# Copying attention's results later, and on VectorE in one chunk, with the gated rows turned one slot later

## The chip, the cores and the metric

The kernel runs on one core of a Trainium2 chip. The metric is the device time of one execution in microseconds (us); lower is better.

## What is computed

Two residual layers on 1024 tokens with 1024 features, in float32. The first is a pooling mixer with a gate. The second, which matters here, is dilated attention with 8 heads of 128 and three groups g of dilations (1, 4, 16):

```python
q = rotary(rms_norm(qkv[:, :, g, 0], q_norm[g]), pos, ROPE_DIM, ROPE_THETA)
k = rotary(rms_norm(qkv[:, :, g, 1], k_norm[g]), pos, ROPE_DIM, ROPE_THETA)
o, lse = dilated_window_attention(q, k, qkv[:, :, g, 2], dil, window // (2 * dil))
...
weights = jax.nn.softmax(jnp.stack(lses, axis=0), axis=0)
o = jnp.einsum('gbsh,gbshe->bshe', weights, jnp.stack(outs, axis=0))
y = o.reshape(B, S, ATT_WIDTH).astype(h.dtype) * jax.nn.silu(gate)
return y @ w_out
```

## The kernel before

All projections come first; attention starts at about 1361 us of the span and lasts to the end. It is cut into six chunks, each of four heads (a half) and one group, in the order `CHUNKS = ((0, 0), (1, 0), (0, 1), (0, 2), (1, 1), (1, 2))`. A chunk has 8 query blocks of 128 rows. A *step* t is one query block of a chunk (t from 0 to 47, and eight more to drain); it has four *slots* h, one for each head, numbered n = 4t + h. The fourth chunk is steps 24 to 31. Its group needs one key block for each query block; groups 0 and 1 need two.

Every engine runs the same loop over n, in an order written out by hand, and waits on semaphores. In slot n TensorE turns the probabilities of head n-3 (L1489, `transpose_p`), makes the scores of head n (L1481, `scores`; called S in the text) and the value product of head n-4 (L1509, `values`). VectorE copies the turned probabilities of head n-3 out of PSUM (L2162, `take_pt`), then adds the mask and takes the row maximum of head n (L2153, `row_max`). ScalarE takes the exponential of head n (L2672, `exps`).

Around that, once in a step: TensorE turns the next step's queries (slot 0) and a block of the next chunk's keys (slot 2, in steps 33 to 38 slot 3), both at L1439 and both into PSUM bank 2; ScalarE copies them out (`take_queries` L2616, `take_keys` L2664) in the same slots, behind the exponential. ScalarE copies the results of a step, four heads in one PSUM bank of 512 columns, to SBUF (`take_u`, L2686).

A half is merged when its third chunk is there. From step 34 (rows 0 to 7) and step 44 (rows 8 to 15) on, one row block m a step is merged: VectorE weighs (L2201) and GpSimd adds and gates (from m = 12 on VectorE and ScalarE do it). One step later TensorE turns the gated rows, also into bank 2 (`turn_gated`, L1439 with `turn` or `turnh_f` as the source); ScalarE copies this out rounded (`y_high`, L2699), VectorE writes the remainder (`y_low`, L2222). One step after that come two half products with the output weight (`project_out`, in slots 0 and 2, 12 products of 512 columns each), which VectorE adds to the residual (L2231). The products of rows 6 and 7 are spread over slot 0 of steps 42 to 45 instead, so these steps have none in slot 2; nor has step 35. ScalarE (L2707) and VectorE (L2237) also split the output weights in steps 40 to 44, and in steps 42, 44, 46 and 48 they make merging factors.

A turn into bank 2 waits until the last contents are copied out:

```python
def bank2_free():
    for ready, n in zip((kt_copied, qt_copied, ylo_done), turned):
        if n:
            pe.wait_ge(ready, n)
```

Of the kernel before, what the change touches and what calls it, by code (L numbers as in the profile page):

```python
# [37 lines left out]
def encoder_program(nc, x, pool_norm, pool_w_in, pool_w_group, pool_scale, pool_w_out, att_norm, att_w_in,  # L38
# [3 lines left out]
    TB, KD = T // P, D // P  # L42
# [92 lines left out]
    with ctx:  # L135
# [332 lines left out]
        def group(c):  # L468

            return CHUNKS[c][1]  # L470
# [46 lines left out]
        def row_at(t, lag):  # L517

            found = [m for m in range(NROW) if merge_step(m) + lag == t]
            return found[0] if found else None  # L520
# [28 lines left out]
        def spill_number(c, b):  # L549

            return TB * [n for n in range(NCHUNK) if CHUNKS[n][1] < NA - 1].index(c) + b

        ON_POOL = range(TB + 4)
        ON_SCALAR = range(TB + 4, NROW)

# [7 lines left out]
        def projected(t, h):  # L563

            if (t, h) in SPREAD:
                return SPREAD[t, h]
            m = row_at(t, 2)
            return (m, h // 2) if h in (0, 2) and m is not None and m not in SPREAD_ROWS else None
# [615 lines left out]
        def _(pe):  # L1184
# [308 lines left out]
            def values(n):  # L1493
                c, h, b = block_of(n)
                t = n // HALF
                if h == 0:
                    if b == 0 or (b == 4 and c == NCHUNK - 1):
                        before_now = [x for x in range(c + 1) if x % 2 == c % 2]
                        wide = sum(CHUNKS[x][1] == 0 for x in before_now)
                        if b == 0:  # L1500
                            pe.wait_ge(v_in[c % 2][0], 16 * len(before_now))
                        if b == 4 or c < NCHUNK - 1:
                            pe.wait_ge(v_in[c % 2][1], 16 * (len(before_now) + 2 * wide))
                    if t >= 2:
                        pe.wait_ge(u_evac, t - 1)
                pe.wait_ge(pt_ready, n + 1)
                vb = value_blocks(group(c), b)
                for i, v in enumerate(vb):
                    last = nc.tensor.matmul(value_bank(t)[:, P * h:P * h + P], pt[:, n % 4, P * i:P * i + P],  # L1509
                                            v_rows[c % 2][v // 4][:, v % 4, HD * h:HD * h + HD], start=(i == 0),  # L1510
                                            stop=(i == len(vb) - 1))
                last.then_inc(pv_done, 1)
# [36 lines left out]
            for n in range(HALF * END):  # L1549
                t, h = n // HALF, n % HALF  # L1550
                if 0 <= n - LAG < NHEAD:
                    transpose_p(n - LAG)
                if n < NHEAD:
                    scores(n)
                if 0 <= n - LAG - 1 < NHEAD:
                    values(n - LAG - 1)
                if projected(t, h):
                    project_out(*projected(t, h))
                if h == 1 and row_at(t, 1) is not None:
                    turn_gated(row_at(t, 1))  # L1560
                if h == 0 and t + 1 < NSTEP:
                    turn_queries(t + 1)
                if h == keys_head(t) and t + TB < NSTEP:
                    turn_keys(t // TB + 1, t % TB)
# [3 lines left out]
        def _(dve):  # L1568
# [587 lines left out]
            def take_pt(n):  # L2156
# [4 lines left out]
                    dve.wait_ge(pv_done, n - 3)  # L2161
                nc.vector.tensor_copy(pt[:, n % 4, 0:kn], bank(3 + n % 2)[:, 0:kn]).then_inc(pt_ready, 1)  # L2162

            def factor_terms(half, first, n):

                at = slice(first, first + n)
                s = [st0[:, half, at], st1[:, half, at], stat[:, last_chunk(half), at]]
                for g in range(2):
                    dve.wait_ge(st_in[g], 16 * (half + 1))
                dve.wait_ge(p_done, HALF * (TB * last_chunk(half) + first + n))  # L2170
                link(nc.vector.tensor_tensor(fmin[:, at, :], s[0][:, :, 0, :], s[1][:, :, 0, :], ALU.min))
                link(nc.vector.tensor_tensor(fmin[:, at, :], fmin[:, at, :], s[2][:, :, 0, :], ALU.min))
                for g in range(NA):
                    last = nc.vector.tensor_tensor(fac[:, g, at, :], fmin[:, at, :], s[g][:, :, 0, :], ALU.subtract)
                last.then_inc(f_sub, 1)
# [64 lines left out]
            for n in range(HALF * END):  # L2240
                t, h = n // HALF, n % HALF
                if projected(t, h - 1):
                    add_rows(*projected(t, h - 1))
                if 0 <= n - LAG < NHEAD:
                    take_pt(n - LAG)
                if n < NHEAD:
                    row_max(n)
                if h == 0 and t in FACTORS:
                    factor_terms(*FACTORS[t])
                if h == 2 and row_at(t, 1) is not None:  # L2250
                    y_low(row_at(t, 1))
                if row_at(t, 0) is not None:
                    merge(row_at(t, 0), h)
                if h == 3 and t in FACTORS:
                    factors(*FACTORS[t])
                if n - 2 in OUT_SPLITS:
                    out_low(OUT_SPLITS[n - 2])
# [3 lines left out]
        def _(act):  # L2261
# [413 lines left out]
            def take_u(t):  # L2675

                c, b = t // TB, t % TB
                act.wait_ge(pv_done, HALF * (t + 1))
                if group(c) == NA - 1:
                    place = v_rows[1][b // 4][:, b % 4, :]  # L2680
                else:
                    n = spill_number(c, b)
                    if n >= 4:
                        act.wait_ge(u_out[n % 4], 16 * (n // 4))
                    place = ub[:, n % 4, :]
                nc.scalar.activation(place, value_bank(t), ACT.Copy).then_inc(u_evac, 1)  # L2686
# [34 lines left out]
            for n in range(HALF * END):  # L2721
                t, h = n // HALF, n % HALF
                if n < NHEAD:
                    exps(n)
                if h == 1 and row_at(t, 1) is not None:
                    y_high(row_at(t, 1))
                if h == 0 and row_at(t, 0) in ON_SCALAR:
                    scale_heads(row_at(t, 0), 3)
                if h > 0 and row_at(t, -1) in ON_SCALAR:
                    scale_heads(row_at(t, -1), h - 1)  # L2730
                if h == 0 and t + 1 < NSTEP:
                    take_queries(t + 1)
                if h == 1 and t in FACTORS:
                    exp_factors(*FACTORS[t])
                if h == 3 and 1 <= t <= NSTEP:
                    take_u(t - 1)
                if h == keys_head(t) and t + TB < NSTEP:
                    take_keys(t // TB + 1, t % TB)
                if n in OUT_SPLITS:
                    out_high(OUT_SPLITS[n])  # L2740
# [52 lines left out]
```

## Time and profile before

| what | value |
|---|---|
| runs | 1683.63 us median of 3 (1682.88 to 1683.65) |
| profiled execution | 1682.04 us, span 1680.2 us |
| TensorE matmul busy | 1656.5 us, 99% of the span |
| VectorE, ScalarE, GpSimd busy | 1148.6, 837.6, 269.6 us |
| granted TensorE clock | 1.0 |

The profile follows one execution; times of rows are us from the start of its span. "Busy" of TensorE uses modelled ends of products. The idle time in brackets at the end of a row is what the engine stood idle ahead of it, and what released it. PE is TensorE, DVE VectorE, ACT ScalarE, POOL GpSimd, SPq the queue of SyncE that issues the transfers.

### The profile page before, as it was taken

How to read it: one execution, taken by the hardware profiler on the slowest of the kernel's cores; microseconds unless marked ns; L12 is line 12 of the kernel's file. 1: busy time of each engine (PE TensorE's matmuls, PEld its weight loads, DVE VectorE, ACT ScalarE, POOL GpSimd, SP SyncE). 2: the span in 40 equal slices, each digit the busy share in tenths (PEclk: the TensorE clock that was granted, in tenths of full speed). 3: DMA queues.
4: the chain of work that ended last, by engine and by line, in shares of the span. 5: the costliest groups of instructions: out<-in, count | busy, mean ns of one | idle time of the engine just before them, and what ended most of it. 6: DMA issues, size and time to landing. Idle time of an engine off the chain costs nothing.

```text
span 1680.2 us, 23792 instructions
## 1 busy us (share of the span) xinstructions
PE 1656.5 (99%) x8294; PEld 1404.1 (84%) x8294; DVE 1148.6 (68%) x1962; ACT 837.6 (50%) x1948; POOL 269.6 (16%) x292
## 2 busy tenths in 40 slices
PE   8999999999999999999999999999999999999999
PEld 8888888778888878888888888888888889999877
DVE  5885677677985687586868356774468336666575
ACT  6453333432441463475655246573456268885453
POOL 2000000004312100141423013240023000004440
PEclk9999999999999999999999999999999999999999
DMA  6133333484411424332332414332334646767774
GB/s 191 51 125 127 123 102 101 151 321 155 175 49 52 143 103 145 106 120 83 125 117 84 155 61 155 107 114 88 125 112 140 230 165 220 251 212 228 256 264 156
DMA packets 146276, 243.12 MB, mean 145 GB/s; under 512 B 17264, under 2 KB 55152, under 8 KB 145136
## 3 DMA queue, kind: packets, MB, share of 16 engines
q1 hardware_dynamic: 141264, 224.31, 39.9%
q10 hardware_dynamic: 4896, 17.30, 2.8%
q8 instruction: 68, 1.11, 0.3%
q14 instruction: 48, 0.39, 0.1%
HBM read 161.75 MB, written 79.82 MB: 144 GB/s over the span
## 4 chain that ended last, share of the span: by engine, by line
PE 91%; DVE 4%; DMA 2%; issue 1%; ACT 1%; SPq 0%; ACTq 0%; POOL 0%; DVEq 0%
PE pair L1186 26%; PE pair L1188 26%; PE pair L1187 26%; PE pair L1509 4%; PE pair L1481 3%; PE pair L1439 3%; PE pair L1489 2%; DMA ubuf<-diff_spill 1%; DMA raw<-in_pool_w_out_dram 1%; PE pair L1207 1%; DMA xs<-in_x_dram 0%; DMA raw<-in_pool_w_in_dram 0%; DVE w L1586 0%; DVE w L1669 0%; DVE hTl L1757 0%
## 5 line engine op out<-in xcount | busy, mean ns | idle before, releaser
L1186 PE MATMUL pair<-w,turnh 128*128 128x512 f32 x640 | 249.0, 389 | 0.0
L1187 PE MATMUL pair<-w,turnh 128*128 128x512 f32 x640 | 249.0, 389 | 0.0
L1188 PE MATMUL pair<-w,turnl 128*128 128x512 f32 x640 | 249.0, 389 | 0.0
L1186 PE MATMUL pair<-w,hTh 128*128 128x512 f32 x544 | 214.0, 393 | 2.2 <-DVE xs L1675 2.2
L1188 PE MATMUL pair<-w,hTl 128*128 128x512 f32 x544 | 212.0, 390 | 0.0
L1187 PE MATMUL pair<-w,hTh 128*128 128x512 f32 x544 | 211.7, 389 | 0.0
L2591 ACT ACTIVATE both<-pair 128x512 f32<-128x512 f32 x160 | 94.3, 592 | 177.8 <-PE pair L1188 166.9
L2089 DVE TENSOR_TENSOR both<-pair,both 128x512 f32<-128x512 f32 x120 | 81.5, 686 | 112.0 <-PE pair L1188 111.4
L2602 ACT ACTIVATE dump<-both 128x128 f32<-128x128 f32 x384 | 119.4, 311 | 64.0 <-DVE both L2089 51.4
L1186 PEld LDWEIGHTS pair<-w,turnh 128*128 128x128 f32 x640 | 120.1, 188 | 25.0
L1187 PEld LDWEIGHTS pair<-w,turnh 128*128 128x128 f32 x640 | 120.1, 188 | 25.0
L1188 PEld LDWEIGHTS pair<-w,turnl 128*128 128x128 f32 x640 | 120.1, 188 | 24.9
L1154 POOL TENSOR_SCALAR qvar<-qss 128x4 f32<-128x4 f32 x96 | 41.5, 432 | 539.8 <-ACT dump L2602 536.9
L1186 PEld LDWEIGHTS pair<-w,hTh 128*128 128x128 f32 x544 | 102.2, 188 | 22.9 <-DVE xs L1675 2.5
L1188 PEld LDWEIGHTS pair<-w,hTl 128*128 128x128 f32 x544 | 102.1, 188 | 21.5
L2672 ACT ACTIVATE pp<-pp,stat 128x256 f32<-128x256 f32 (+2 forms) x192 | 86.8, 452 | 66.4 <-DVE stat L2153 64.9
L1187 PEld LDWEIGHTS pair<-w,hTh 128*128 128x128 f32 x544 | 102.2, 188 | 20.6
L2162 DVE COPY pt<-pair 128x256 f32<-128x256 f32 (+1 forms) x192 | 72.5, 378 | 50.3 <-PE pair L1489 47.0
L1142 POOL TENSOR_TENSOR diff<-stage,diff 128x1024 fp32r<-128x1024 f32 x12 | 42.3, 3556 | 388.9 <-ACT diff L2486 388.9
L1159 POOL TENSOR_TENSOR qrstd<-qvar,neg_half 128x4 f32<-128x4 f32 x96 | 100.9, 1051 | 8.0
L1186 PE MATMUL pair<-hTh,w 128*128 128x512 f32 (+1 forms) x280 | 99.5, 355 | 2.7 <-DVE hTl L1757 1.9
L1187 PE MATMUL pair<-hTl,w 128*128 128x512 f32 (+1 forms) x280 | 98.7, 353 | 0.0
(241 smaller groups left out, 3819.1 us busy)
## 6 DMA issues: line engine op xcount, KB each, us to landing
part_spill<-both SPq DMA_DIRECT2D x160, 256.0 KB, 3.6
both<-part_spill SPq DMA_DIRECT2D x22, 1024.0 KB, 6.6
raw_z<-in_att_w_in_dram SPq DMA_DIRECT2D x20, 1024.0 KB, 5.3
raw<-in_pool_w_in_dram SPq DMA_DIRECT2D x32, 512.0 KB, 5.7
raw<-in_att_w_in_dram SPq DMA_DIRECT2D x10, 1024.0 KB, 6.2
raw_u<-in_att_w_in_dram SPq DMA_DIRECT2D x10, 1024.0 KB, 5.7
diff_spill<-ubuf SPq DMA_DIRECT2D x16, 512.0 KB, 2.6
stage<-gate_spill SPq DMA_DIRECT2D x16, 512.0 KB, 6.1
```

The costliest lines, as they stand in the source:

```text
L1159: nc.gpsimd.tensor_tensor(qrstd[:, z % 4, :], qvar[:, z % 4, :], neg_half[:, :], ALU.pow).then_inc(a_rstd, 1)
L1186: nc.tensor.matmul(out, lh, rh, start=first, stop=False, skip_group_check=onto)
L1187: nc.tensor.matmul(out, lh, rl, start=False, stop=False, skip_group_check=onto)
L1188: return nc.tensor.matmul(out, ll, rh, start=False, stop=last, skip_group_check=onto)
L1439: last = nc.tensor.transpose(out[:, P * h:P * h + P], rows[:, P * h:P * h + P], ident[:, :])
L1481: nc.tensor.matmul(out, qT[:, b % 2, h, :], keys(c, b, h), start=True, stop=True).then_inc(s_done, 1)
L1509: last = nc.tensor.matmul(value_bank(t)[:, P * h:P * h + P], pt[:, n % 4, P * i:P * i + P], v_rows[c % 2][v // 4][:, v % 4, HD * h:HD * h ...
L2089: nc.vector.tensor_tensor(place, bank(source), place, ALU.add).then_inc(a_added, 1)
L2162: nc.vector.tensor_copy(pt[:, n % 4, 0:kn], bank(3 + n % 2)[:, 0:kn]).then_inc(pt_ready, 1)
L2591: nc.scalar.activation(place, bank(4 + p if i == 3 else p), ACT.Copy).then_inc(a_kept, 1)
L2602: nc.scalar.activation(dump[:, :], x4[:, h, :], ACT.Square, accum_out=qss[:, z % 4, h:h + 1]).then_inc(a_sq, 1)
L2672: nc.scalar.activation(pp[:, n % 4, at], pp[:, n % 4, at], ACT.Exp, bias=stat[:, c, b, 0, h:h + 1], scale=-1.0, accum_out=stat[:, c, b, 1, ...
```

## The change

The copy of a step's results stands at slot 3 of the next step; it now stands at slot 1 of the step after that. In the fourth chunk (`ON_VECTOR`) VectorE makes it, behind its row maximum. `turn_gated` moves from slot 1, behind the output product if there is one, to slot 2, ahead of it, and `y_high` from slot 1 to slot 2, behind the exponential; `y_low` was in slot 2 already.

```diff
+        ON_VECTOR = range(TB * CHUNKS.index((0, NA - 1)), TB * CHUNKS.index((0, NA - 1)) + TB)
...
                     values(n - LAG - 1)
+                if h == 2 and row_at(t, 1) is not None:
+                    turn_gated(row_at(t, 1))
                 if projected(t, h):
                     project_out(*projected(t, h))
-                if h == 1 and row_at(t, 1) is not None:
-                    turn_gated(row_at(t, 1))
...
+            def take_u(t):
+
+                b = t % TB
+                dve.wait_ge(pv_done, HALF * (t + 1))
+                if t == ON_VECTOR.start:
+                    dve.wait_ge(u_evac, t)
+                nc.vector.tensor_copy(v_rows[1][b // 4][:, b % 4, :], value_bank(t)[:, :]).then_inc(u_evac, 1)
...
                     row_max(n)
+                if h == 1 and t - 2 in ON_VECTOR:
+                    take_u(t - 2)
...
                 act.wait_ge(pv_done, HALF * (t + 1))
+                if t == ON_VECTOR.stop:
+                    act.wait_ge(u_evac, t)
...
-                if h == 1 and row_at(t, 1) is not None:
+                if h == 2 and row_at(t, 1) is not None:
                     y_high(row_at(t, 1))
...
-                if h == 3 and 1 <= t <= NSTEP:
-                    take_u(t - 1)
+                if h == 1 and 2 <= t <= NSTEP + 1 and t - 2 not in ON_VECTOR:
+                    take_u(t - 2)
```

How this stands on the engines, at the three places of which the text below speaks. The lines of the changed kernel are up to 13 numbers higher.

VectorE in a step of the fourth chunk, before the change, slots 1 and 2: a copy of turned probabilities, and a row maximum in two instructions.

```order
L2162 COPY pt<-pair 128x128
L2153 ISA pp,stat<-pair,both 128x128
L2153 ISA stat 128x1
L2162 COPY pt<-pair 128x128
L2153 ISA pp,stat<-pair,both 128x128
```

The same place in the changed kernel (`turn` is where the group's results go).

```order
L2163 COPY pt<-pair 128x128
L2154 ISA pp,stat<-pair,both 128x128
L2154 ISA stat 128x1
L2171 COPY turn<-pair 128x512
L2163 COPY pt<-pair 128x128
L2154 ISA pp,stat<-pair,both 128x128
```

The 512 column copy has come between the row maximum of slot 1 and the copy of slot 2.

TensorE in step 42 before: the query turn that ends slot 0, slot 1 with the gated turn, slot 2.

```order
L1439 MATMUL pair<-ident,both 128x128 x4
L1489 MATMUL pair<-ident,pp 128x128
L1481 MATMUL pair<-turnh_f,qT 128x128
L1509 MATMUL pair<-turn,pt 128x128
L1439 MATMUL pair<-ident,turnh_f 128x128 x4
L1489 MATMUL pair<-ident,pp 128x128
L1481 MATMUL pair<-turnh_f,qT 128x128
L1509 MATMUL pair<-turn,pt 128x128
```

And now.

```order
L1440 MATMUL pair<-ident,both 128x128 x4
L1490 MATMUL pair<-ident,pp 128x128
L1482 MATMUL pair<-turnh_f,qT 128x128
L1510 MATMUL pair<-turn,pt 128x128
L1490 MATMUL pair<-ident,pp 128x128
L1482 MATMUL pair<-turnh_f,qT 128x128
L1510 MATMUL pair<-turn,pt 128x128
L1440 MATMUL pair<-ident,turnh_f 128x128 x4
```

The gated turn has moved behind the second head.

ScalarE in step 42 before, from the exponential of slot 1 on: y_high, the factors' exponential, a weights' copy, the exponentials of slots 2 and 3, the results copy.

```order
L2672 ACTIVATE pp,stat<-pp,stat 128x128
L2699 ACTIVATE hTh<-pair 128x512
L2692 ACTIVATE fac<-fac 128x3x8
L2707 ACTIVATE turnl<-raw 128x512
L2672 ACTIVATE pp,stat<-pp,stat 128x128 x2
L2686 ACTIVATE turn<-pair 128x512
```

And now (here L2699 is the results copy and L2712 is y_high).

```order
L2683 ACTIVATE pp,stat<-pp,stat 128x128
L2705 ACTIVATE fac<-fac 128x3x8
L2699 ACTIVATE turn<-pair 128x512
L2720 ACTIVATE turnl<-raw 128x512
L2683 ACTIVATE pp,stat<-pp,stat 128x128
L2712 ACTIVATE hTh<-pair 128x512
```

y_high has moved behind the exponential of slot 2, and the results copy has come ahead of both.

## Rows read from the trace of the kernel before

**Rows 1.** Stretch, length, busy us (xcount) of PE, PEld, DVE, ACT, POOL; clock, DMA.

```profile
1440.00:1480.00 40.00, 40.00 (x330) 39.76 (x328) 26.35 (x107) 32.16 (x93) 0.00 (x0) 1.00 0.69 228
1500.00:1510.00 10.00, 9.43 (x83) 8.95 (x81) 6.62 (x36) 9.73 (x32) 0.00 (x0) 1.00 0.53 185
```

**Rows 2.** Timeline, fourth chunk, one period: start, duration, engine, instruction.

```profile
1492.60 0.63 PE L1439 MATMUL pair<-ident,both 128*128 128x128 f32 x4 [0.19 <-issue]
1493.18 0.39 PE L1481 MATMUL pair<-turnh_f,qT 128*128 128x128 f32 x2
1493.27 0.69 ACT L2664 ACTIVATE turn<-pair,lead 128x512 f32<-128x512 f32 x1
1493.71 0.29 DVE L2153 CUSTOM_DVE_ANT_0 pp<-pair,both 128x128 f32<-128x128 f32 x1
1494.05 0.40 ACT L2672 ACTIVATE pp<-pp,stat 128x128 f32<-128x128 f32 x1
1494.18 0.60 PE L1439 MATMUL pair<-ident,both 128*128 128x128 f32 x4
1494.45 0.58 ACT L2686 ACTIVATE turn<-pair 128x512 f32<-128x512 f32 x1
1495.31 0.67 ACT L2616 ACTIVATE qT<-pair,lead 128x512 f32<-128x512 f32 x1
1496.08 0.63 PE L1439 MATMUL pair<-ident,both 128*128 128x128 f32 x4 [0.19 <-issue]
```

**Rows 3.** Timeline, VectorE: copies of 128 and of 256 columns.

```profile
1499.30 0.29 DVE L2162 COPY pt<-pair 128x128 f32<-128x128 f32 x1
1499.51 0.28 DVE L2153 CUSTOM_DVE_ANT_0 pp<-pair,both 128x128 f32<-128x128 f32 x1
...
1517.35 0.42 DVE L2162 COPY pt<-pair 128x256 f32<-128x256 f32 x1
```

**Rows 4.** Timeline, last keys' copy ahead of the fifth chunk, its first scores.

```profile
1510.65 0.69 ACT L2664 ACTIVATE turn<-pair,lead 128x512 f32<-128x512 f32 x1
1511.44 0.56 PE L1481 MATMUL pair<-turn,qT 128*128 128x192 f32 x2 [0.16 <-issue]
```

**Rows 5.** Timeline, steps 33 and 34: results copy, keys' copy, query turn.

```profile
1520.46 0.58 ACT L2686 ACTIVATE ub<-pair 128x512 f32<-128x512 f32 x1
1520.94 0.68 ACT L2664 ACTIVATE turnh_f<-pair,lead 128x512 f32<-128x512 f32 x1
...
1521.67 0.55 PE L1439 MATMUL pair<-ident,both 128*128 128x128 f32 x3 [0.34 <-ACT turnh_f L2664]
```

**Rows 6.** Timeline, step 35: VectorE's weighing, y_low, key turn.

```profile
1526.71 1.96 DVE L2201 TENSOR_TENSOR both<-both,fac 128x1024 f32<-128x1024 f32 x1
...
1530.37 0.69 DVE L2222 TENSOR_TENSOR hTl<-pair,hTh 128x512 fp32r<-128x512 f32 x1
...
1531.31 0.63 PE L1439 MATMUL pair<-ident,both 128*128 128x128 f32 x4 [0.16 <-issue]
```

**Rows 7.** Timeline, step 42: query turn, exponential, gated turn, value product.

```profile
1598.08 0.60 PE L1439 MATMUL pair<-ident,both 128*128 128x128 f32 x4
...
1599.49 0.40 ACT L2672 ACTIVATE pp<-pp,stat 128x128 f32<-128x128 f32 x1
1599.51 0.63 PE L1439 MATMUL pair<-ident,turnh_f 128*128 128x128 f32 x4 [0.27 <-issue]
...
1601.86 0.35 PE L1509 MATMUL pair<-turn,pt 128*128 128x128 f32 x1 [0.28 <-DVE pt L2162]
```

**Rows 8.** Timeline, step 45: exponential of slot 2, value product behind slot 3.

```profile
1621.07 0.40 ACT L2672 ACTIVATE pp<-pp,stat 128x128 f32<-128x128 f32 x1 [0.33 <-DVE stat L2153]
...
1621.98 0.46 PE L1509 MATMUL pair<-turnh_f,pt 128*128 128x128 f32 x2 [0.28 <-DVE pt L2162]
```

**Rows 9.** Timeline, step 48: value product of slot 2.

```profile
1644.37 0.49 PE L1509 MATMUL pair<-turnh_f,pt 128*128 128x128 f32 x2 [0.17 <-DVE pt L2162]
```

**Rows 10.** The statistics' tile: time from issue to landing of its four loads.

```profile
DMA to landing us min/median/max: 2.2/6.6/7.7
```

## The prediction

> **What bounds the kernel now.** I read the stretches first. While the third chunk runs (1440 to 1480 us) TensorE is busy in all of its 40 us and ScalarE in 32; in the fourth chunk (1500 to 1510) TensorE shows 9.43 of 10 and ScalarE 9.73 [rows 1]. So nearly everywhere TensorE's own work is the time, and only its waits can be changed; both edits lie in the last 190 us. Then I read the timeline, one step at a time, and looked on TensorE for turns and value products that carry an idle time. The ends of its products are modelled, so the idle printed is smaller than the stall; I take stalls from the starts.
>
> The fourth chunk has one key block for each query block. From a key turn at 1492.60 to the query turn at 1494.18 TensorE needs 1.58 us (a turn and two heads; a turn is about 0.45, a head 0.56); from there to the next key turn, the same work, it takes 1.90 [rows 2]. The 0.32 is a stall. What closes the circle of 3.48 us (1492.60 to 1496.08) is ScalarE: key turn, S 0.58 later, VectorE's row maximum 0.53 later, exponential 0.34, copy of the results 0.40, then exponential and copy of the queries 0.86 after that copy began, whose 0.67 us end releases the key turn [rows 2]. The results copy L2686 is on this circle with some 0.47 us.
>
> **The change, part by part.** Of the fourth chunk's copies, eight go from ScalarE to VectorE; all others stay on ScalarE and move from slot 3 to slot 1 of the next step, where nothing waits for them in chunks 1 to 3, since TensorE is full there [rows 1]. No instruction is added but waits.
>
> (a) *Fourth chunk.* VectorE has no row for a copy of 512 columns from PSUM. Its copies of 128 and 256 columns last 0.29 and 0.42, 0.13 for 128 more; after one of 128 the next instruction starts 0.21 later [rows 3], so one of 512 holds the queue for 0.21+3x0.13 = 0.60 (0.68 if all of its duration counts: the upper bound; 0.5, if its cost per column were a little less, the lower). The new copy stands in slot 1 behind the row maximum; queued behind it are the probabilities' copy and the row maximum of slot 2, behind these ScalarE's exponential of slot 2 and its copy of the keys, and TensorE's next query turn waits for that copy, as both turns use bank 2. The circle that this makes: query turn to S of slot 1 0.58, to row maximum 0.53, to the new copy 0.21, to the probabilities' copy 0.60, to the maximum 0.21, to the exponential 0.34, to the keys' copy 0.40 [rows 2, 3], to the query turn 0.73 (1520.94 to 1521.67) [rows 5]: 3.60 us. That is more than the 3.48 of now. ScalarE's relief is real, but the last arrival is now the keys' copy instead of the queries'. Five periods (steps 26 to 31) cost 5x0.12 = 0.6, the step before some 0.1. At the seam, S of the fifth chunk waits for the last keys' copy: 0.79 after its start [rows 4]. That start is 1.90+0.67 = 2.57 after the query turn now and 3.60-0.73 = 2.87 then: +0.3. Together **+1.0** (0.4 to 1.5 with 3.5 to 3.68 for the circle). [...]
>
> (b) *Steps 33 and 34.* Here the keys are turned in slot 3, and ScalarE's results copy stood ahead of the keys' copy: 1520.46, then 1520.94, then the query turn 1521.67 with a printed wait [rows 5]. Moved away, the keys' copy starts 0.48 earlier: **-0.5**. In step 34 the same wait stands, but VectorE is then inside its 1.96 us product L2201 (from 1526.71) [rows 6], and the value product behind the query turn waits for it: nothing gained (at best another 0.5).
>
> (c) *Step 35.* Turning the gated rows in slot 2 puts ScalarE's y_high behind the exponential of that slot and behind the results copy that now stands in slot 1: 0.47 us for the copy and some 0.45 for the exponential later. y_low starts at 1530.37 now and the key turn that waits for it at 1531.31 [rows 6]. In step 35 there is no output product to cover it: **+0.8** (0.5 to 0.95).
>
> (d) *Steps 36 to 41, and 46.* With an output product of 12 wide matmuls behind the turn, y_high and y_low are covered. What goes: in steps 41, 42, 45 and 46 the gated turn in slot 1 waits for the queries' copy of slot 0. Query turn 1598.08, gated turn 1599.51, 1.43 apart for 1.00 of work [rows 7]; the row stands at 1589.99, 1618.89 and 1626.47 too. 0.43 us each. Steps 41 and 46 keep it, the latter less what a late VectorE copy takes, and 0.1 comes in step 40: **-0.8**. In 42 and 45 it is swallowed by the next term.
>
> (e) *Steps 42 and 45* have a gated turn and no product in slot 2. VectorE then stands in y_low until y_high is done, and the probabilities' copy of slot 3 is queued behind it, for which the value product of the next slot waits. Step 42: ScalarE's exponential of slot 1 starts at 1599.49 [rows 7]; 0.40 for it, 0.2 (an estimate) for that of the factors, 0.47 results copy, 0.6 weights' copy (as wide as that of the results, 0.58 [rows 2]), 0.4 exponential of slot 2 put y_high at 1601.55; y_low 0.62 later (y_high is as wide, too), the copy 0.60 after that, the value product 0.33 after that (0.29 and a semaphore): 1603.1, where it is 1601.86 now [rows 7]: +1.2. Step 45: the exponential of slot 2 starts at 1621.07 because VectorE's maximum does, and this is not changed; 0.40+0.62+0.60+0.33 behind it is 1623.0, now 1621.98 [rows 8]: +1.05. Together **+2.25** (1.5 to 2.6).
>
> (f) *Steps 47 and 48* turn no queries. The value product of slot 2 waits for VectorE there, as at 1644.37 [rows 9], and the gated turn, which filled that wait, now comes behind it: 0.35 (step 47, where less is waited) and 0.45: **+0.8** (0 to 0.9). From step 49 on no heads are left, and the order of turns and products is the old one: nothing.
>
> Sum: 1.0-0.5+0.8-0.8+2.25+0.8 = **+3.5 us**. It is made on an execution of 1682.04 (span 1680.2); the median of the three runs is 1683.63, 1.6 above. On the median: **1687.2 us**.
>
> **Rivals.** *VectorE is never last.* It is busy 6.6 us of 10 in the fourth chunk [rows 1]. If the copy and y_low fit into its idle time, then ScalarE's relief counts in full: the fourth chunk falls to TensorE's own 3.1 to 3.2 us a step (-0.3x6, seam -0.3), -0.5, four gated waits (-1.7): -4.3, 1679.3 us, faster. It decides whether in the fourth chunk the keys' copy starts less than 0.85 after the key turn. Against it: the slack there is small, the keys' copy could start only 0.18 later than now (1493.27+0.73 against 1494.18) [rows 2]. Chance 0.1.
> *The copy is absorbed, the y stalls are not*: with a circle near 3.2, (a) becomes -2, and the sum +0.5: 1684.1. Chance 0.12.
> *The y stalls are small*: if ScalarE reaches y_high early, terms (c) and (e) vanish and 42 and 45 keep their 0.43: sum about -0.4, 1683.2. Against it, ScalarE issues in order and the exponential of slot 2 needs VectorE. Chance 0.1.
> *SyncE's queue.* Step 39's results are now copied in slot 1 of step 41 instead of slot 3 of step 40, and SyncE's last load of the statistics stands behind their store. Such loads landed 2.2 to 7.7 us after their issue [rows 10]; VectorE wants this one in slot 0 of step 42, an estimated 4.5 us after its new issue. With the longest landing it is up to 3 us more, 1690. Chance 0.08.
>
> **Numbers.** My forecast has 0.6, with its own range 1685.3 to 1688.9 from the bounds of (a), (c), (e) and (f), not all at one end. The whole range, 1682.8 to 1689.0, takes in the second and third rival. 0.2% of 1683.63 is 3.4 us, about what a measurement of this kernel tells from no change; the forecast lies on that border. So slower 0.45, same 0.45, faster 0.1.
>
> **What would show it.** (a) In the fourth chunk the idle stands before the query turns, not the key turns, and these are 3.6 us apart; the keys' copy starts about 1.27 after its turn. (b) 1521.67's wait is gone. (c) to (e): no idle before gated turns; VectorE waits for hTh in steps 35, 42 and 45, and the value product behind it idles by over 1.5 us in 42. It would be wrong if VectorE's copy lets the queue go in under 0.5 us, or if some stall of mine is taken up by a wait that stands there anyway.

## The result and the profile after

| | before | changed |
|---|---|---|
| median of 17 runs each, side by side | 1682.91 us (1681.71 to 1684.27) | 1686.95 us (1684.30 to 1688.78) |
| profiled execution, span | 1682.04, 1680.2 us | 1685.22, 1683.4 us |
| matmul, VectorE, ScalarE busy | 1656.5, 1148.6, 837.6 us | 1655.7, 1151.4, 834.7 us |

The ratio is 1.0022 (95% interval 1.0016 to 1.0028): 4.0 us slower in the medians, 3.2 in the two profiled executions, both at a mean granted clock of 1.0. Three executions far off all others are left out of the ranges and ratios below: one each of two variants, at a mean clock of 0.75 and 0.56, and one of the kernel before that took 5555 us. The two differences, 4.0 and 3.2, turn out to have different causes. First the 3.2.

The stretches of [rows 1] in the changed kernel:

```profile
1440.00:1480.00 40.00, 40.00 (x330) 39.77 (x329) 26.30 (x109) 31.96 (x93) 0.00 (x0) 1.00 0.71 235
1500.00:1510.00 10.00, 9.21 (x79) 8.64 (x78) 7.15 (x37) 8.28 (x30) 0.00 (x0) 1.00 0.62 224
```

In the fourth chunk ScalarE has been relieved, by 1.45 us in 10, and TensorE, which is what counts, does less than before. The timeline of one period (beside [rows 2]), with all lines that make up the circle:

```profile
1494.69 0.66 PE L1440 MATMUL pair<-ident,both 128*128 128x128 f32 x4 [0.26 <-ACT turn L2675]
...
1496.04 0.69 DVE L2171 COPY turn<-pair 128x512 f32<-128x512 f32 x1
1496.29 0.60 PE L1440 MATMUL pair<-ident,both 128*128 128x128 f32 x4
...
1496.64 0.28 DVE L2163 COPY pt<-pair 128x128 f32<-128x128 f32 x1
...
1496.84 0.28 DVE L2154 CUSTOM_DVE_ANT_0 pp<-pair,both 128x128 f32<-128x128 f32 x1
...
1497.17 0.40 ACT L2683 ACTIVATE pp<-pp,stat 128x128 f32<-128x128 f32 x1 [0.51 <-DVE stat L2154]
1497.57 0.67 ACT L2675 ACTIVATE turn<-pair,lead 128x512 f32<-128x512 f32 x1
...
1498.29 0.66 PE L1440 MATMUL pair<-ident,both 128*128 128x128 f32 x4 [0.26 <-ACT turn L2675]
```

The new copy lasts 0.69 us, and the next instruction on VectorE starts 0.60 after it. ScalarE now stands idle 0.51 waiting for VectorE's row maximum, the keys' copy is late, and the idle of TensorE has moved from the key turns to the query turns, which are 3.60 us apart.

Steps 34 and 35, the turns and the product on VectorE (beside [rows 5, 6]):

```profile
1522.48 0.66 PE L1440 MATMUL pair<-ident,both 128*128 128x128 f32 x4
...
1527.39 0.66 PE L1440 MATMUL pair<-ident,both 128*128 128x128 f32 x4
1527.52 1.45 DVE L2210 TENSOR_TENSOR both<-both,fac 128x1024 f32<-128x1024 f32 x1
...
1530.99 0.58 ACT L2712 ACTIVATE hTh<-pair 128x512 fp32r<-128x512 f32 x1
1531.60 0.69 DVE L2231 TENSOR_TENSOR hTl<-pair,hTh 128x512 fp32r<-128x512 f32 x1 [1.41 <-ACT hTh L2712]
1532.54 0.63 PE L1440 MATMUL pair<-ident,both 128*128 128x128 f32 x4 [1.04 <-DVE hTl L2231]
```

The two query turns have lost their wait (the second stood at 1527.06 before, below); the key turn behind `y_low` has 1.04 us where it had 0.16.

```profile
1527.06 0.65 PE L1439 MATMUL pair<-ident,both 128*128 128x128 f32 x4 [0.34 <-ACT turnh_f L2664]
```

Step 42 (beside [rows 7]), step 45 ([rows 8]) and the tail ([rows 9]):

```profile
1601.44 0.39 ACT L2683 ACTIVATE pp<-pp,stat 128x128 f32<-128x128 f32 x1
1601.83 0.58 ACT L2712 ACTIVATE hTh<-pair 128x512 fp32r<-128x512 f32 x1
1602.44 0.69 DVE L2231 TENSOR_TENSOR hTl<-pair,hTh 128x512 fp32r<-128x512 f32 x1 [1.53 <-ACT hTh L2712]
1603.05 0.28 DVE L2163 COPY pt<-pair 128x128 f32<-128x128 f32 x1
...
1603.47 0.46 PE L1510 MATMUL pair<-turn,pt 128*128 128x128 f32 x2 [1.89 <-DVE pt L2163]
...
1624.76 0.46 PE L1510 MATMUL pair<-turnh_f,pt 128*128 128x128 f32 x2 [1.41 <-DVE pt L2163]
...
1642.83 0.46 PE L1510 MATMUL pair<-turnh_f,pt 128*128 128x128 f32 x2 [0.41 <-DVE pt L2163]
...
1647.11 0.49 PE L1510 MATMUL pair<-turnh_f,pt 128*128 128x128 f32 x2 [0.61 <-DVE pt L2163]
```

In steps 42 and 45 this is one chain: the exponential of slot 2, the upper half on ScalarE, the lower half on VectorE, the probabilities' copy queued behind it, the value product. In step 35 the same chain ends in the key turn instead, which waits for the lower half. The last two rows are another matter. The wait of 0.41 stands in the kernel before as well, and the 0.61 is the 0.17 of [rows 9], grown because the gated turn that filled part of it now comes behind it.

```profile
1640.09 0.46 PE L1509 MATMUL pair<-turnh_f,pt 128*128 128x128 f32 x2 [0.41 <-DVE pt L2162]
```

The table of TensorE's waits of the whole execution agrees: waits for `pt` 3.2 us before (first line), 6.6 after.

```profile
PE pair L1509 <- DVE pt L2162: 3.2, 8, 1.3
...
PE pair L1510 <- DVE pt L2163: 6.6, 9, 1.9
```

### The profile page after: what moved, and what is told of

Same layout as the page of the kernel before. It is cut to its first block, busy times and chain, and to the rows that moved or that the text cites. A ratio compares the mean times of both kernels' runs of the same rounds, so it can differ in the third digit from the quotient of the medians.

```text
span 1683.4 us, 23793 instructions
## 1 busy us (share of the span) xinstructions
PE 1655.7 (98%) x8294; PEld 1404.1 (83%) x8294; DVE 1151.4 (68%) x1970; ACT 834.7 (50%) x1940; POOL 270.7 (16%) x292
## 4 chain that ended last, share of the span: by engine, by line
PE 91%; DVE 4%; issue 1%; DMA 1%; ACT 1%; SPq 0%; ACTq 0%; POOL 0%; DVEq 0%
PE pair L1187 26%; PE pair L1189 26%; PE pair L1188 26%; PE pair L1510 4%; PE pair L1482 3%; PE pair L1440 3%; PE pair L1490 2%; DMA raw<-in_pool_w_out_dram 1%; PE pair L1208 1%; DMA xs<-in_x_dram 0%; DVE pt L2163 0%; DMA raw<-in_pool_w_in_dram 0%; ACT pp L2683 0%; DVE hTl L1758 0%; DVE w L1587 0%
```

## The experiments

Three batches on three chips. Besides the medians I compare the steps' starts in the traces (by ScalarE's copy of the queries, L2616 and its equals, one a step; "steps 24 to 32" is from the copy in step 24 to that in step 32), and the executions at a mean clock of 1.0, for a reason that the first batch shows. In the 96 runs of the kernel before that stood beside the experiments, 44 had a mean clock of 1.0 (median 1682.0) and 52 of 0.999 (1683.5), none less.

**Copy back on ScalarE.** All copies two steps behind, none on VectorE.

```diff
-                if h == 1 and t - 2 in ON_VECTOR:
-                    take_u(t - 2)
...
-                if h == 1 and 2 <= t <= NSTEP + 1 and t - 2 not in ON_VECTOR:
+                if h == 1 and 2 <= t <= NSTEP + 1:
```

> The changed kernel with the fourth chunk's copies back on ScalarE (slot 1, two steps behind); the gated turn stays in slot 2. Theory 1 (the VectorE copy closes a circle of 3.60 us through the keys' copy, and the gated turn makes the stalls of steps 35, 42 and 45): the period of steps 26 to 31 falls to about 3.45 us (query turn, S 0.58, maximum 0.53, exponential 0.34, results copy 0.40, exponential 0.47, keys' copy 0.40, query turn 0.73), and the kernel stays about 1.9 us over the kernel before: 1684.8. Theory 2 (moving ScalarE's copies to slot 1 is what costs, wherever they are made): no gain over the changed kernel, 1687, and chunks 1 to 3 show waits of TensorE that the kernel before has not.

Measured: 1687.04 (1685.76 to 1687.94), ratio 1.0024 (1.0015 to 1.0034). Steps 24 to 32 took 29.37 us, against 28.73 before and 29.85 in the changed kernel: the steps were 3.46, but for one of 3.82, whose row maximum began 0.36 late for no reason that the trace shows, and the fifth chunk still began late. So of the 1.1 us that the fourth chunk lost, taking the copy off VectorE gives back 0.5, or 0.8 without that one step, but not all. The expectation's second theory, that the place of the copies on ScalarE is what costs, is out: steps 0 to 23 take 116.42 us in all three kernels. But the time, expected at 1684.8, is off by 2.2. At the same mean clock the variant is a little faster than the changed kernel (at 0.999 1686.1 against 1687.0, at 0.998 1687.9 against 1688.3), yet none of its nine executions had 1.0. In this profile the step from the queries' copy of step 42 to that of 43 took 9.59 us, where it took 8.01 in the changed kernel's profile, with the same wait of 1.90 in it.

**Gated turn undone.** `turn_gated` and `y_high` in slot 1 as before, the VectorE copy kept.

```diff
-                if h == 2 and row_at(t, 1) is not None:
-                    turn_gated(row_at(t, 1))
                 if projected(t, h):
                     project_out(*projected(t, h))
+                if h == 1 and row_at(t, 1) is not None:
+                    turn_gated(row_at(t, 1))
...
-                if h == 2 and row_at(t, 1) is not None:
+                if h == 1 and row_at(t, 1) is not None:
                     y_high(row_at(t, 1))
```

> The changed kernel with gated turn and y_high back in slot 1, behind the output product; the VectorE copy stays. Theory 1: the waits at about 1532.5, 1603.5 and 1621.2 to 1624.8 us go back to their old size, and 0.4 us waits ahead of the gated turns return; period of the fourth chunk 3.60 still. Sum against the kernel before +1.1 for the fourth chunk, -1.0 for steps 33 and 34: +0.1 to +0.4, 1683.2. Theory 2 (the copies' place costs everything): 1686 to 1687.

Measured: 1683.10 (1681.92 to 1684.23), ratio 1.0002 (0.9993 to 1.0011), period still 3.60. The loss in the fourth chunk (24 to 32: 29.84) stays, steps 32 to 46 take 111.79 instead of 114.28 (before: 112.80). The moved turn is the larger price; the copies of the other chunks, two steps behind, gain 1.0 in steps 33 to 35.

**Turn moved only where covered.** In slot 2 in steps 36 to 41 and 46, where a half product stands behind it, else in slot 1.

```diff
+        def gated_slot(t):
+            return 2 if projected(t, 2) and t < NSTEP - 1 else 1
...
-                if h == 2 and row_at(t, 1) is not None:
+                if h == 2 and h == gated_slot(t) and row_at(t, 1) is not None:
                     turn_gated(row_at(t, 1))
                 if projected(t, h):
                     project_out(*projected(t, h))
+                if h == 1 and h == gated_slot(t) and row_at(t, 1) is not None:
+                    turn_gated(row_at(t, 1))
...
-                if h == 2 and row_at(t, 1) is not None:
+                if h == gated_slot(t) and row_at(t, 1) is not None:
                     y_high(row_at(t, 1))
```

> The changed kernel, but the gated turn and y_high stand in slot 2 only in steps in which an output product follows there (36 to 41 and 46), and in slot 1 in all others. Theory 1: the losses of 42 and 45 (1.2 us each in the profile after) and of step 35 go, the gain of step 41 (0.5) and of 46 (0.3) stays: 0.5 to 1.0 us under the kernel before in spite of the 3.60 us circle, 1682.2. If the cover of the output product does not matter: the same as with the turn undone.

Measured: 1681.85 (1680.85 to 1683.35), ratio 0.9996 (0.9987 to 1.0005); steps 32 to 46 take 111.00. Where the cover is there, the moved turn is a gain: 0.8 us in these steps of the trace, and 0.2 more in step 46 (from there to the last addition 51.11 us, 51.35 with the turn undone).

**VectorE copy in slot 2** instead of slot 1, ahead of slot 3's queue and behind the row maximum for which the keys' copy waits.

```diff
-                if h == 1 and t - 2 in ON_VECTOR:
+                if h == 2 and t - 2 in ON_VECTOR:
                     take_u(t - 2)
```

> The changed kernel with VectorE's copy one slot later, behind the row maximum of slot 2, where TensorE turns the keys. Theory 1: neither the exponential of slot 2 nor that of slot 0 is behind the copy now; the period falls to 3.1 to 3.2 us, the fourth chunk is 2 us faster than in the kernel before instead of 1.1 slower, and the kernel comes out at 1683.0 to 1683.8, since the gated turn's stalls stay. Rival (VectorE's queue is simply too full in this chunk, wherever the copy stands): period 3.5 to 3.6 and no change, 1687.

Measured: 1684.37 (1682.92 to 1686.73), ratio 1.0009 (1.0 to 1.0018); 1683.8 at a clock of 1.0, the top of what was expected. The period is 3.18, TensorE's own work, and steps 24 to 32 take 27.28. Nearly a microsecond of it is given back in steps 33 and 35 (4.33 and 9.92 us, 3.97 and 9.30 in the changed kernel). In step 35 VectorE's product (L2210) lasts 2.08 us instead of 1.45, and the value product behind the query turn waits:

```profile
1528.52 0.49 PE L1510 MATMUL pair<-turn,pt 128*128 128x128 f32 x2 [0.41 <-DVE pt L2163]
```

And this profile, too, has 9.60 us from step 42 to 43. Here is why. TensorE in it behind the wait of step 43, and the stretches around it (length, busy PE, clock, DMA):

```profile
1602.64 0.46 PE L1510 MATMUL pair<-turn,pt 128*128 128x128 f32 x2 [1.89 <-DVE pt L2163]
...
1603.86 0.39 PE L1188 MATMUL pair<-w,hTh 128*128 128x512 f32 x1
1604.09 0.57 PE L1189 MATMUL pair<-w,hTl 128*128 128x512 f32 x1
1604.46 0.63 PE L1187 MATMUL pair<-w,hTh 128*128 128x512 f32 x1
1604.89 0.63 PE L1188 MATMUL pair<-w,hTh 128*128 128x512 f32 x1
```

```profile
1602.00:1604.00 2.00, 1.36 (x7) 1.00 1.03 321
1604.00:1606.00 2.00, 2.00 (x7) 0.53 0.98 322
1606.00:1608.00 2.00, 2.00 (x10) 0.61 0.96 387
1608.00:1610.00 2.00, 2.00 (x20) 1.00 1.06 414
```

The products go from 0.23 to 0.43 us apart: the granted clock has fallen to half, some 1.5 us after the wait ended (in slices of 0.25 us it is 0.50 from 1604.25 to 1607.50, 0.77 and 0.90 in the slices beside, and 1.00 before and behind). The same two stretches in the changed kernel's own profile:

```profile
1604.00:1606.00 2.00, 2.00 (x10) 1.00 0.97 253
1606.00:1608.00 2.00, 2.00 (x18) 1.00 0.98 403
```

So the stall of step 43, which the gated turn of step 42 makes, costs 1.2 us (from step 42 to 43, 8.01 us in the changed kernel's profile for 6.81 before) and in some executions 1.6 more (9.60). There is a second such place in every kernel here, in front of the attention layer's first product, where the kernel before waits, too (2.25 us). In the profile of the variant with the turn where covered (idle 2.27 us ahead of 590.65):

```profile
588.00:590.00 2.00, 0.38 (x4) 1.00 0.67 165
590.00:592.00 2.00, 1.35 (x5) 0.87 1.07 390
592.00:594.00 2.00, 2.00 (x7) 0.50 0.94 268
594.00:596.00 2.00, 2.00 (x13) 0.77 1.02 399
```

and in the kernel before (idle 2.25 us ahead of 591.08), with the clock staying up:

```profile
590.00:592.00 2.00, 0.92 (x4) 1.00 1.03 387
592.00:594.00 2.00, 2.00 (x11) 1.00 0.94 277
594.00:596.00 2.00, 2.00 (x15) 1.00 1.01 376
```

The next eight kernels were chosen for this as much as for the sum.

**Both parts re-placed**: copy in slot 2, turn only where covered.

> The changed kernel with both parts re-placed: VectorE copies the fourth chunk's results in slot 2 instead of slot 1, and the gated row is turned in slot 2 only in the steps where a second half product stands behind it (36 to 41 and 46), in slot 1 in all others. Theory (two independent terms): the copy in slot 2 gave 1.45 us in the fourth chunk against the kernel before, the turn where it is covered 1.8 us over steps 32 to 46 in a profile and 1.0 in the median; together 1680.0 us (1679.3 to 1681.0) where the kernel before has 1682.9. Rival (the two share a gain, since the row that ScalarE is late with after the fourth chunk is the one that the moved turn relieves): 1681.8, no better than the moved turn alone.

Measured: 1681.01 (1679.06 to 1681.60), ratio 0.9988 (0.9979 to 0.9997), the upper end of what was expected. At a clock of 1.0 1679.5, 2.5 below the kernel before, but seven of its ten executions had 0.999. The earlier fourth chunk gives back as much as with the turn in slot 2: in step 35 0.65 (9.02, and 8.37 with the turn alone re-placed), there 0.62. So the terms add.

**Upper half ahead of the exponential** of slot 2 on ScalarE, in all steps.

```diff
+                if h == 2 and row_at(t, 1) is not None:
+                    y_high(row_at(t, 1))
                 if n < NHEAD:
                     exps(n)
-                if h == 2 and row_at(t, 1) is not None:
-                    y_high(row_at(t, 1))
```

> The changed kernel with ScalarE taking the upper half of the turned gated row ahead of the exponential of the same slot 2, instead of behind it, in all steps. Theory (what TensorE waits for in steps 35, 42, 45 and 48 is the chain turn, exponential, upper half, lower half, copy of the turned probabilities, value product): each of these stalls gets shorter by 0.3 to 0.4 us, some of it given back where the exponential is now late in the covered steps: 1685.6 us (1684.8 to 1686.5) where the changed kernel has 1687. Rival (the stall is VectorE's own work, the order on ScalarE does not matter, or the late exponential costs as much): 1687.

Measured: 1683.41 (1683.01 to 1685.66), ratio 1.0007 (0.9998 to 1.0017). The waits of steps 35, 42 and 45 fall:

```profile
1533.68 0.63 PE L1440 MATMUL pair<-ident,both 128*128 128x128 f32 x4 [0.62 <-DVE hTl L2231]
...
1604.29 0.46 PE L1510 MATMUL pair<-turn,pt 128*128 128x128 f32 x2 [1.47 <-DVE pt L2163]
...
1624.75 0.46 PE L1510 MATMUL pair<-turnh_f,pt 128*128 128x128 f32 x2 [0.60 <-DVE pt L2163]
```

By 0.42, 0.42 and 0.81, together 1.65 us; those of 1642.83 and 1647.11 are unchanged. At a clock of 1.0 the variant has 1683.2, 2.0 under the 1685.2 of the changed kernel's seven such executions. The stalls of these three steps are the chain through ScalarE, not VectorE's own work, and the two others are not this chain. The median is below the expected range of 1684.8 to 1686.5, for two reasons. I had put the gain in step 45 too low, since there the exponential itself waited 0.32 us for VectorE. And with 1.47 us of idle none of 11 executions was at 0.998. That alone proves little, as another variant that keeps the 1.89 us (the half copy, below) had one of 11. The profile, taken at a clock of 0.999, had its fall at the second place (0.50 over 592 to 594 us) and 1.00 from 1600 to 1610.

**Stall of step 43 filled** with 14 turns of the identity (their results are overwritten).

```diff
+                if (t, h) == (43, 0):
+                    pe.wait_ge(out_added, 13)
+                    for i in range(14):
+                        nc.tensor.transpose(bank(0)[:, P * (i % 4):P * (i % 4) + P], ident[:, :], ident[:, :])
                 if 0 <= n - LAG - 1 < NHEAD:
                     values(n - LAG - 1)
```

> The changed kernel with 14 turns of the identity (some 1.6 us of TensorE, into the bank that the next half product overwrites) ahead of the value product at which TensorE waits 1.89 us in step 43. Their results are not used. Theory of the clock (in some executions the granted clock falls to the lower level right behind that idle stretch, as in the profiles of two variants, 0.57 and 0.61 over 1604 to 1608 us, and costs some 1.6 us there): the stall stays as long, but is no longer idle, the clock stays up, and the slower executions become fewer: median 1685.6 (1684.9 to 1686.2). Rival (the clock falls by itself, whatever TensorE did before): 1687.0, with the same spread of 1684.3 to 1688.8. If the turns take longer than the stall, up to 0.3 more in either.

Measured: 1686.62 (1684.48 to 1687.02; 1686.35 without the execution at 0.56 of the clock), ratio 1.0021 (1.0012 to 1.0030). The median missed the expected 1684.9 to 1686.2; the top end is 1.8 below the changed kernel's, and no execution is at 0.998. Eight of ten were at 0.999, though. By the median alone this is inconclusive: the second place had been left open.

**Step 42 too.** The gated turn in slot 2 where covered, and in step 42 (`return 2 if t == 42 or ...`).

> The variant with the gated row turned in slot 2 only where a half product covers it, plus step 42, where none does (the copy on VectorE in slot 1, as in the changed kernel). Against the variant without step 42 (1681.85) this isolates one stall. Theory: 1.2 us more in every execution, and the clock drop of 1.6 us behind it in a part of them: 1683.05 in an execution without the drop, median 1683.8 (1683.0 to 1684.8). Rival (a single stall is caught up by the steps behind it, the loss needs several in a row): within 0.3 us of 1681.85.

Measured: 1684.81 (1681.91 to 1685.79), ratio 1.0009 (1.0 to 1.0018), that is 3.0 more than without step 42 (on another chip, where the kernel before had 0.2 more). Five executions of 11 stood at 0.998 (median 1685.5), four at 0.999 (1684.1), two at 1.0 (1682.0, against 1681.4 without step 42). In the trace step 42 to 43 takes 9.59 for 6.83, that is 1.2 for the stall and 1.6 for the clock, and nothing of it is caught up: the three steps behind take 5.54, 6.98 and 7.65 us, for 5.53, 6.96 and 7.64. One stall does this. My 1683.8 was too low, as the lower clock came more often than I had assumed. The two executions at 1.0 are only 0.6 above those without step 42, or 0.9 with the difference of the chips; they are two.

**Both idle stretches filled** in the changed kernel: the 14 turns, and 16 ahead of the attention layer's first product, by

```diff
+            pe.wait_ge(*released(("O", 1, 5)))
+            for i in range(16):
+                nc.tensor.transpose(bank(4)[:, P * (i % 4):P * (i % 4) + P], ident[:, :], ident[:, :])
             pe.wait_ge(o_added, NQ + 2 * TB)
```

> The changed kernel with useless turns of the identity in the two idle stretches of TensorE that are about 2 us long: 14 in step 43 (idle 1.89 us) and 16 ahead of the attention layer's first product (idle 2.28 us near 590 us, in the kernel before as well). Their results are not used. Theory (the executions at 0.999 and 0.998 of the full clock are those in which it fell to the lower level behind one or both of these idle stretches): the executions come together at a mean clock of 1.0, median 1685.2 (1684.5 to 1685.7), none above 1686.3. Rival (the drops come whatever TensorE did before): half the executions stay at 0.999, median 1686.6.

**Before, filled**: the kernel before with these 16 turns alone.

> The kernel before the change, with 16 useless turns of the identity in the idle 2.28 us near 590 us. By the clock theory its executions at 0.999 disappear: median 1681.9 (1681.5 to 1682.4) where the kernel before has 1682.9. Beside the changed kernel with both stretches filled it gives the change's price without the clock: 3.2 us, as in the two profiles at a clock of 1.0. Rival: 1682.9, and the difference stays at 4.

**Both parts re-placed, filled**: the copy in slot 2, the turn where covered, the 16 turns.

> The variant with both parts re-placed (copy in slot 2, turn only where covered), and 16 useless turns of the identity in the idle 2.28 us near 590 us. By the clock theory the half of the executions that ran 1.6 us longer is gone: median 1679.5 (1679.0 to 1680.2), ratio 0.998 to the kernel before. Rival (no effect of the filling): 1681.0 as without it.

| | median | range | ratio to before | executions at 1.0 |
|---|---|---|---|---|
| changed, both filled | 1684.87 | 1684.12 to 1685.74 | 1.0012 (1.0003 to 1.0022) | 11 of 11 |
| before, filled | 1682.22 | 1681.45 to 1682.49 | 0.9995 (0.9986 to 1.0004) | 11 of 11 |
| re-placed, filled | 1679.57 | 1679.09 to 1680.05 | 0.9980 (0.9971 to 0.9989) | 11 of 11 |
| before, beside them | 1683.03 | 1680.89 to 1684.49 | | 13 of 32 |

The first in the timeline, and its clock, where the 2.28 us were:

```profile
588.00 1.03 PE L1208 MATMUL pair<-ident,both 128*128 128x128 f32 x8
588.88 1.91 PE L1535 MATMUL pair<-ident 128*128 128x128 f32 x16
```

```profile
588.00:590.00 2.00, 2.00 (x20) 1.00 0.64 172
590.00:592.00 2.00, 1.46 (x11) 1.00 0.96 370
592.00:594.00 2.00, 2.00 (x11) 1.00 0.97 307
```

All three medians came out as expected, and 33 executions of 33 ran at 1.0. The useless turns in the idle stretches of TensorE have taken away the loss behind them. The difference of changed and before is 2.65 us with the stretches filled (I had expected 3.2) and 4.0 without: about 1.4 of the result was the clock's. Among executions at 1.0 alone it is 3.2 (1685.2 and 1682.0), which would leave the clock 0.8; the runs do not decide between the two. The last variant is 3.5 us below the kernel before, the best found; 0.8 of it is the filling alone.

**Half of the copy.** VectorE copies only columns 0 to 255 of each 512; the others are left out.

```diff
-                nc.vector.tensor_copy(v_rows[1][b // 4][:, b % 4, :], value_bank(t)[:, :]).then_inc(u_evac, 1)
+                nc.vector.tensor_copy(v_rows[1][b // 4][:, b % 4, 0:256], value_bank(t)[:, 0:256]).then_inc(u_evac, 1)
```

> The changed kernel whose VectorE copies only 256 of each 512 columns of the results in the fourth chunk (the other half is left out). Theory (the step of 3.60 us there is a circle through VectorE in which the copy's time counts in full): the step falls by what 256 columns are shorter, 0.17 to 0.19 us, to 3.41 to 3.43, and the end by 8 of them, 1.4 us: 1685.5 in the median. Rival (the step is set by the copy's place in the queue, by its wait or its fixed part, and not by its length): 3.58 to 3.60, 1687.

Measured: 1684.37 (1682.77 to 1685.95), ratio 1.0010 (1.0001 to 1.0019); 1683.1 at a clock of 1.0.

```profile
1494.23 0.66 PE L1440 MATMUL pair<-ident,both 128*128 128x128 f32 x4
...
1495.59 0.42 DVE L2171 COPY turn<-pair 128x256 f32<-128x256 f32 x1
...
1495.92 0.28 DVE L2163 COPY pt<-pair 128x128 f32<-128x128 f32 x1
...
1497.57 0.66 PE L1440 MATMUL pair<-ident,both 128*128 128x128 f32 x4
```

The copy holds VectorE for 0.33 instead of 0.60, and the step, 3.60, is 3.33: the whole 0.27 passes through, six times (steps 23 to 32 take 32.89 us for 34.50). That is the prediction's circle, shown by taking a piece out of it. The figure that I expected, 0.17 to 0.19, was a slip: the spacing of [rows 3] gives 0.21 + 0.13 = 0.34 for 256 columns, so 0.26; hence the median below the expected 1685.5.

## Why the prediction was right, point by point

The time (1687.2) was 0.25 us above the measured 1686.95, and slower was right. But the two do not consist of the same parts. (The terms of the prediction add up to 3.55, written as 3.5.) From the starts of the queries' copies, changed minus before:

| stretch | term | predicted | measured |
|---|---|---|---|
| steps 23 to 32 | (a) | +1.0 | 34.50 - 33.44 = +1.06 |
| 32 to 35 | (b) | -0.5 | 13.90 - 14.86 = -0.96 |
| 35 to 36 | (c) | +0.8 | 9.30 - 8.42 = +0.88 |
| 36 to 42 | (d), steps 40 and 41 | -0.5 | 61.77 - 62.55 = -0.78 |
| 42 to 46 | (e) | +2.25 | 29.31 - 26.97 = +2.34 |
| 46 to the last addition | (f), and step 46 of (d) | +0.5 | 51.74 - 51.34 = +0.40 |
| sum | | +3.5 | +2.94 |

Another 0.24 had arisen ahead of the attention, where nothing was changed (steps 0 to 23 take 116.42 us in both); with it the two profiled executions differ by 3.18.

(a) Right, down to its parts. By the query turns, 0.15 was lost ahead of step 26, 0.62 in the five periods and 0.29 at the seam (0.1, 0.6 and 0.3 were said); circle 3.60; the copy's hold 0.60; the keys' copy 1.28 after the key turn (1.27 was said), the query turn 0.72 behind it (0.73). The half copy shows that the length of the copy sets the circle, the copy in slot 2 that its place does. The price is only there because it stands between the row maximum of slot 1 and that of slot 2. The bound of 0.68 from its whole duration does not come into play: in the rows above the next copy starts 0.60 after the start of one that lasts 0.69.

(b) The step that failed, by its size: "nothing gained (at best another 0.5)" in step 34. It gained 0.49 (4.90 for 5.39). VectorE's product, which was to stand in the way for 1.96 us, lasted 1.45 there, begun 0.13 behind the query turn; so it ended 1.58 us behind that turn, for 1.61 before, and took nothing back. The copy in slot 2 shows the mechanism of which the prediction thought: there the product lasted 2.08, and step 35 gave back 0.62. What sets its length was not tested. In the traces it lasts 1.22 or 1.23 with GpSimd idle and 1.37 to 2.09 where a product of GpSimd overlaps it. In the kernel before it took 1.96 beside one of 1.04 that had begun 0.17 ahead of it, now 1.45 beside one that began 0.33 behind it and took 2.02.

(c) Right, 0.88 in the bounds of 0.5 to 0.95; the wait of 1.04 names `hTl` as its releaser, as expected.

(d) Right where it was counted: step 41 gained 0.49 (0.43 was said), step 40 0.13 (0.1). Steps 36 to 38 gained another 0.15, uncounted.

(e) Right: +1.20 in step 42 (1.2 was said) and +1.22 in step 45 (1.05). The chain, link by link in step 45, was 0.40, 0.61, 0.61 and 0.43 behind an exponential at 1622.71, for 0.40, 0.62, 0.60 and 0.33. The reversal on ScalarE shows that it is that chain, undoing the turn that the stall belongs to it.

(f) Nearly right, +0.4 with step 46. The turn moved only where covered tells the two apart: it gains 0.23 in step 46 (51.11 for 51.34), so steps 47 and 48 cost 0.63, for 0.8 said.

What the prediction did not have is the clock. Its sum is one of work, 3.5 said and 2.65 to 3.2 measured (2.94 in the table), and the remaining 0.8 to 1.4 of the median's 4.0 is the lower clock, seen in the traces of three variants behind the stall of step 43 (0.50 for 3.4 us). A third error is in the base: the sum was put on a median of three executions, 1683.63, which is 0.7 above the 1682.91 of the seventeen. The change was put 0.5 too low and the base 0.7 too high, and that the rest is only 0.25 is chance. Of 59 executions of kernels that keep this stall unfilled (changed 17, copy on ScalarE 9, copy in slot 2 11, step 42 too 11, half copy 11), 18 have a mean clock of 0.998; of the others whose clock is listed, those of the kernel before among them, none has.

Of the rivals, the first falls, as VectorE was last: the keys' copy starts 1.28 after its turn, and the rival needed under 0.85. The period near 3.2 that the second assumed comes only with the copy in slot 2. The stalls in `y_low` were not small. SyncE's queue did no harm: the last load of the statistics was issued at 1592.3 and landed 2.2 us later, and VectorE took them at 1596.46 without a wait:

```profile
1596.46 0.16 DVE L2180 TENSOR_TENSOR fmin<-st 128x8 f32<-128x8 f32 x1
```

## What to carry to other kernels

Moving work off the busier engine helps only if its new place is off the circle; write the circle down link by link for the new engine's queue, as the relieved engine's idle (here 0.51 us of ScalarE) is no gain. A step that two engines hand on to a third should be moved behind another's work only in those steps in which something covers it, which an order written by hand can tell apart. And a stall of TensorE near 2 us can cost more than its length (1.6 us more in some executions here), so remove or fill it first, and compare executions of one clock before judging tenths of a per cent.

## What the runs showed of the hardware

In five profiles (copy back on ScalarE, turn where covered, copy in slot 2, upper half ahead, step 42 too) the granted clock fell, eight times in all: to 0.50, for 3.4 us, each time between 0.2 us before and 1.5 us after the end of an idle stretch of TensorE of 1.89 or 1.90 us (step 43) or 2.27 to 2.29 us (near 590 us). Products of 512 columns were then 0.43 us apart for 0.23. The cost was 1.6 us in step 43 (9.59 or 9.60 for 8.01 from step 42 to 43) and 1.5 to 1.6 near 590 us (from the first product there to the 25th 8.76 to 8.87 for the 7.27 of the kernel before). In the profiles of the kernel before (2.25 us idle) and of the changed one (2.28 and 1.89 us) it did not fall, so such a stretch does not always bring it. The three profiles with two falls have a mean clock of 0.998, the two with one fall 0.999. Of the runs of the kernel before, 52 of 96 had 0.999; with TensorE kept at turns at the second place none of 11 had, nor of the 22 of the two other filled kernels. After the idle 1.47 us in step 43 none of 11 executions had 0.998, which is weak evidence.
